# GpSimd's split of a weight unit into high and low parts: the low part written in eight blocks of 128x128 in place of four of 128x256

## The reference, cut to what matters

```python
u = rmsnorm(h, norm_mix[i]);  proj = u @ w_in[i]                  # first block, attention and delta-net inputs
h = h + jnp.concatenate([attn_out, dn_out], axis=-1) @ w_o[i]
gate = jax.nn.sigmoid(rmsnorm(h, norm_ple[i]) @ w_ple_gate[i])
h = h + gate * (p[i] @ w_ple_proj[i])
u = h @ w_in[l];  x = x + jnp.concatenate([y_pool, y_hgrn], axis=-1) @ w_out[l]   # second block
```

## Time and profile before

| | |
|---|---|
| median of 3 runs | 2493.02 us (2489.05 to 2496.16) |
| the profiled execution: its own time | 2492.07 us |
| the span of its trace | 2490.3 us |
| TensorE busy | 2387.1 us (96% of the span) |
| VectorE busy | 1842.2 us (74%) |
| GpSimd busy | 1267.7 us (51%) |
| ScalarE busy | 943.6 us (38%) |
| mean granted TensorE clock | 0.99 of full |

### The profile page before, as it was taken

How to read it: one execution, slowest core, us unless ns; L and a number is a source line. 1 busy time by engine, 2 the same in 40 slices (tenths; PEclk the granted TensorE clock), 3 DMA queues, 4 the chain that set the end, 5 groups by cost and what they waited for, 6 DMA issues and landing times.

```text
span 2490.3 us, 38938 instructions
## 1 busy us (share of the span) xinstructions
PE 2387.1 (96%) x15284; PEld 1893.9 (76%) x15284; DVE 1842.2 (74%) x2356; ACT 943.6 (38%) x1488; POOL 1267.7 (51%) x1143
## 2 busy tenths in 40 slices
PE   8888999999999999999999999999999999999997
PEld 6766777777778877878777778787777877778885
DVE  3676565647877898888946777778487777888887
ACT  3154223315333344344424344444153333444433
POOL 4622333545555545544467656556655555455442
PEclk9998999999999999999999999999999999999998
DMA  4200101210444474434122111111314444744432
GB/s 156 77 18 18 36 22 33 85 52 32 142 142 163 156 255 169 169 111 143 52 68 85 54 35 35 35 44 49 107 40 148 161 149 147 239 163 152 136 126 95
DMA packets 109709, 254.99 MB, mean 102 GB/s; under 512 B 9312, under 2 KB 9568, under 8 KB 107360
## 3 DMA queue, kind: packets, MB, share of 16 engines
q1 hardware_dynamic: 104112, 233.82, 27.7%
q10 hardware_dynamic: 5424, 18.75, 2.2%
HBM read 182.28 MB, written 67.63 MB: 100 GB/s over the span
## 4 chain that ended last, share of the span: by engine, by line
PE 32%; DVE 12%; issue 3%; ACT 1%; POOL 1%; DMA 1%; SPq 0%; DVEq 0%; ACTq 0%; POOLq 0%
PE pairs L687 22%; PE mid L687 10%; DVE work L1757 2%; DVE tmp L1757 2%; DVE res L1757 2%; DVE work_r L1757 2%; DMA w_raw<-w_up 1%; DVE w_raw L1757 1%; DVE tmp L2176 1%; DVE work L2143 1%; POOL w_hi L650 0%; DVE x_lo L1761 0%; POOL w_lo L654 0%; DVE res L2632 0%; DVE x_lo_raw L1757 0%
## 5 line engine op out<-in xcount | busy, mean ns | idle before, releaser
L687 PE MATMUL pairs<-x_hi,w_hi 128*128 128x512 f32 x1592 | 544.5, 406 | 31.8 <-DVE x_lo L1761 14.0
L687 PE MATMUL pairs<-x_lo,w_hi 128*128 128x512 f32 x1592 | 528.6, 396 | 0.5 <-issue 0.5
L687 PE MATMUL pairs<-x_hi,w_lo 128*128 128x512 f32 x1592 | 525.4, 394 | 1.1 <-issue 1.1
L687 PEld LDWEIGHTS pairs<-x_hi,w_hi 128*128 128x128 f32 x1592 | 285.4, 190 | 117.0 <-issue 37.7
L670 POOL TENSOR_TENSOR w_lo<-w_raw,w_hi 128x512 fp32r<-128x512 f32 x150 | 237.9, 1595 | 221.2 <-ACT w_hi L1284 221.1
L687 PEld LDWEIGHTS pairs<-x_hi,w_lo 128*128 128x128 f32 x1592 | 297.9, 189 | 64.5 <-issue 1.2
L687 PEld LDWEIGHTS pairs<-x_lo,w_hi 128*128 128x128 f32 x1592 | 297.0, 189 | 62.5 <-issue 1.3
L687 PE MATMUL pairs<-work_r,w_hi 128*128 128x512 f32 x1072 | 330.1, 392 | 5.1 <-DVE work_r L1757 2.1
L687 PE MATMUL mid<-work_r,w_hi 128*128 128x512 f32 x992 | 311.2, 395 | 17.0 <-DVE work_r L1757 12.1
L654 POOL TENSOR_TENSOR w_lo<-w_raw,w_hi 128x256 fp32r<-128x256 f32 x312 | 314.6, 1039 | 6.5
L647 POOL TENSOR_TENSOR idle<-idle 128x1 f32<-128x1 f32 x78 | 20.1, 258 | 563.6 <-PE pairs L687 554.7
(11 more groups left out here) (217 smaller groups left out, 3876.0 us busy)
## 6 DMA issues: line engine op xcount, KB each, us to landing
h_ops<-work SPq DMA_DIRECT2D x224, 256.0 KB, 4.4
w_raw<-w_stream SPq DMA_DIRECT2D x81, 512.0 KB, 3.5
w_raw<-w_up SPq DMA_DIRECT2D x120, 256.0 KB, 3.9
out_sq<-h_ops SPq DMA_DIRECT2D x28, 1024.0 KB, 5.1
x_lo_raw<-h_ops SPq DMA_DIRECT2D x28, 1024.0 KB, 5.1
work<-w_down SPq DMA_DIRECT2D x16, 1024.0 KB, 6.7
out_sq<-w_down SPq DMA_DIRECT2D x8, 1024.0 KB, 7.3
x_lo_raw<-w_down SPq DMA_DIRECT2D x8, 1024.0 KB, 5.4
```

What stands on the lines that cost most here:

```text
L687: return nc.tensor.matmul(out, w, x, start=start, stop=stop)
```

## The change

The four instructions that write `w_lo` in `split` become eight, of 128 columns each. The last one raises `w_split` as before. The four that write `w_hi` stay as they are, as does every wait.

```diff
             PIECES = [slice(n * QUARTER, (n + 1) * QUARTER) for n in range(4)]
+            TILES = [slice(n * P, (n + 1) * P) for n in range(KT)]
...
-                for part in PIECES:
+                for part in TILES:
                     ins = nc.gpsimd.tensor_tensor(w_lo[:, slot, part], w_raw[:, slot, part], w_hi[:, slot, part], ALU.subtract)
                 ins.then_inc(w_split, 1)
```

## The result

The changed kernel takes **2500.05 us** (median of 19 runs, 2495.25 to 2511.14). The kernel before, in the same comparison, takes 2492.52 us (19 runs, 2484.60 to 2502.28). The ratio is **1.003 [1.002, 1.004]**, so the change costs 7.5 us, with an interval of 5 to 10. The forecast was +1.2 us, with 2488 to 2502 as its range. The time lies inside the range, at its upper end, but the sum was far too small, and "no change that can be measured" did not come true: 19 runs of each tell the two kernels apart. What holds the time is the width of the range. The profiled execution took 2505.18 us, a slow one of the 19. A second profiled execution of the same kernel took 2498.52 us.

The account below looks back on a forecast made before the run. TensorE's matmuls, with some 100 us of holes, were taken to bound the kernel. The terms 1.5 + 1.1 - 1.0 - 0.4 gave +1.2 us, on the median 2493.02 + 1.2 = 2494.2 us, range 2488 to 2502.

Parts of the forecast that it names:

- The price of an instruction and the quiet split: On GpSimd, 460 ns for a 128-column piece; an undisturbed split grows by 0.57 us, nearly all of it hidden.
- The gate unit: Last four units of the gate product: split grows by 0.57 us, 0.3 us of slack stays, so 0.
- The heads of the earlier trace: Five splits in the heads: 0.57 + 1.2 = 1.8 us later against 1.94 us of slack, so 0, barely.
- The pooling split: Split with 0.24 us of slack, ending at 1399.86: grows by 0.57 + 1.0, TensorE opens the unit about 1.3 us late.
- The first split: Already waited for by TensorE: 0.57 us more, plus 1.0 for meeting the `x_lo` operation, +1.5 us (bounds 0.57 and 2.6).
- 2 x 0.57: Two waited-for splits of the last output product, with no further turns against VectorE: +1.1 us (bounds 1.1 and 3.1).
- This wait takes it up: TensorE's 3.0 us wait for VectorE's `small`, at 1432 us, absorbs the 1.3 us of lateness from near 1400: 0.
- SyncE's reload: Reload of the slot starts later by the split's growth, lands in 3.5 us, is needed over 9 us later: nothing.
- VectorE's gain of 1.4 us: Shorter pieces give VectorE 0.25 us back per old meeting: -1.0 us in the wait for `small`, -0.4 us elsewhere.
- the faster rival: Shorter pieces give VectorE 21 us back, nearly half of it on the path: 2485.6 us, chance 0.08.
- The slower one: Slack of heads and gate used up, pooling lateness not absorbed, VectorE gains nothing: +9.8, 2502.8 us, chance 0.13.
- The third rival: Pieces of 128 overlap wholly, without the fixed cost; quiet splits stay at 2.8 us: 2492.5 us, sharing the forecast's 0.79.

Follow-up runs that it names:

- experiment 2: Kernel before with `w_lo` in eight pieces in all splits but the first, which keeps four: 2497.59 us, ratio 1.0026.
- 11: Kernel before with `w_lo` in eight pieces in the last output product's splits alone, four elsewhere: 2494.90 us, ratio 1.0018.
- experiment 1: Kernel before with `w_lo` in eight pieces in the first split alone, four elsewhere: 2490.87 us against 2490.64, ratio 1.0005.
- 3: Kernel before, `w_lo` still in four pieces, with four one-column additions of two SBUF inputs among them in each split: 2496.45 us, ratio 1.0028.
- 7: Kernel before with `w_lo` in two pieces of 512 columns in all splits: 2494.93 us, ratio 1.0019.
- 8: Kernel before with `w_lo` in one instruction of 1024 columns in all splits: 2499.99 us, ratio 1.0042.
- 4: Kernel before, `w_lo` still in four pieces, with four memsets of 96 columns among them in each split: 2495.38 us, ratio 1.0019.

## Why the prediction was right or wrong

**Right, to 0.1 us.** The price of an instruction and the quiet split: 462 ns and 3.38 us, for 460 and 3.38. The gate unit: slack 0.33 us (0.3 predicted), `tmp` pair 2.88 (2.95), so that a meeting gave VectorE 0.28 us back, not 0.25. The heads of the earlier trace rows: low part from 4.28 to 6.01 us, +1.73 for 1.8, slack 0.2 and no wait. The pooling split: +1.52 for 1.57. The seventh unit of the last output product: the gap between matmuls grew from 0.07 us to 0.63, +0.56 for 0.57. `w_lo` at 395.0 us lies inside the 360 to 400 foretold.

**Wrong, term by term.** The mechanism named there (fixed cost of an instruction, turns with VectorE, TensorE waiting where there is no slack) is what the traces show. The sum failed in the terms below. TensorE's waits on the split were foretold at 4 to 5 us and are 6.6 and 7.5, and the matmul foretold at 21.7 us came at 22.30.

- *The first split*, predicted +1.5: TensorE's wait grew by 1.77 us, within the bound of 2.6. Of the split's growth of 2.12 us, 1.55 are meetings where I counted 1.0.
- *"2 x 0.57" for the last output product.* The second unit's term was mis-sized. I wrote that VectorE goes on with operations that take no turns. That holds for what is in line at the old end, but late pieces meet the `work` operations behind it. The wait grew by 1.43 us in the first profile, by 2.4 in the second (3.58 us) and by 2.1 in experiments 2 and 11.
- *"This wait takes it up"* for the 1.3 us of the pooling split. TensorE waited 0.96 us there and the wait for `small` gave back only 0.3. VectorE did run ahead by 3.3 us in the stretch up to 1410 us, compared with how late TensorE was (7.4 us behind the trace of before), but then stood waiting for ScalarE's `state` and had lost its lead at 1422 us: the row

```profile
1422.40 0.69 DVE L1758 TENSOR_TENSOR state<-state,work 128x512 f32<-128x512 f32 x1 [2.51 <-ACT state L1285]
```

- *SyncE's reload, "nothing".* The prediction looked at when TensorE needs the next unit in the slot. Behind the last split the slot takes `w_up`, which VectorE needs at once. That split grew by 2.35 us (6.18 to 8.53), VectorE waits 1.15 us for the load, and TensorE 1.0 us more for VectorE. The start of the first MLP adds 0.3 and 0.2 us of TensorE's wait for `work` in the two profiles; why is not shown.
- *VectorE's gain of 1.4 us.* VectorE got 16 us of busy time back (21 us were worked out in the faster rival), but TensorE's waits behind it shrank by no more than the 0.3 us of `small`. In the first block's heads it went the other way: three waits for `state`, 1.0 us, where a small VectorE operation in the chain of the recurrence is late.
- *The clock* had no term at all. A longer pause of TensorE can have a stretch at 1.2 GHz behind it, as at 23 and 1747 us. At the first place the clock fell in the three traces with a wait of 2.37 to 2.73 us (the change twice, experiment 1) and stayed up in the eleven with 1.60 us or less. At the second it fell behind waits of 2.62, 3.29 and 3.19 us (the first profile, 2, 3) and stayed up behind 3.58 and 3.31. Over the 19 runs the mean granted clock was 0.9881. Over 93 runs of the kernel before, in the comparisons of the experiments, it was between 0.9895 and 0.9901, and their times rise by about 1700 us per unit of clock lost (correlation -0.68). The cleanest pair is experiment 2 and its own before, 0.9887 and 0.9895. The change's 0.9881 lies 0.0014 to 0.0020 lower. A loss of 0.0008 to 0.0020 is 1.4 to 3.4 us, an estimate from this correlation, not a thing that an experiment separated.

The sum by measured terms, first and second profile of the change: waits on the split +4.8 and +5.7 us, `state` +1.0 and +1.0, `work` at the start of the two MLPs +1.3 and +1.2, `small` -0.3 and -0.4, in all **+6.8 and +7.5 us, beside 7.5 in the runs** (5 to 10). The clock's 1.4 to 3.4 us would come on top, 8.2 to 10.9, and the longer waits for "issue" in the first block with it. The pairs of traces differ by 13.1 and 13.4 us, more than the runs do. So the waits alone are enough, and how much of the clock and of "issue" belongs to the change stays open.

**The rivals.** The slower one gave 2502.8 us, near the 2500.05 measured, but for a reason that didn't happen: no gate unit and no head of the earlier trace rows waits for its split. It shares two of its parts with what happened: the pooling split isn't taken up, and VectorE's gain isn't won. The faster rival fell: waits on VectorE did not shrink. Half of its rule is real all the same, as experiments 7 and 8 show in reverse: longer pieces do cost VectorE time, and TensorE with it. From four pieces to eight VectorE still gains, but TensorE's new waits are more. The third rival fell with the 462 ns.

The exclusive lock of the Trainium skill (SBUF - State Buffer, the section on SBUF's layout and its two sides) agrees with experiments 3 and 4: a one-column addition with two SBUF inputs waits for a whole turn of VectorE, and a memset doesn't.

## What to carry to other kernels

When an operation of GpSimd with two SBUF inputs runs beside a busy VectorE, count turns before elements. Each instruction more costs GpSimd up to one whole VectorE instruction (1.0 us here), each longer one costs VectorE, and the best size lies between (four pieces here, with 0.42%, 0.19% and 0.30% lost at one, two and eight). A split that is late meets what comes next on VectorE, so look past the old end when you size it. Ask of every split what its slot is loaded with next and who waits for that load; the last one before a new stage is easily missed. Allow for a fall of the clock behind a longer pause of TensorE, and don't read a stretch at half clock as the edit's before a kernel unchanged there has been seen without it.

## What was not expected of the hardware

- A one-column addition on GpSimd of 194 ns took 437 ns on average among the pieces (x312), while a memset of 96 columns took 177 ns on average at the same places, also beside VectorE.
- The same instructions, behind the same pause of TensorE (2.25 to 2.27 us, near 475 us of the span), ran at the full clock in five traces and fell to half in nine. Behind a pause of 3.58 us near 1744 us the clock stayed up, and behind one of 2.62 us at the same place it fell. The time at half clock was 44.9 and 52.9 us in two traces of the very same kernel.
- TensorE stood for "issue" inside its stretches of small matmuls for 6.0 to 11.2 us in all, with the longest single one between 1.7 and 2.4 us, differing from execution to execution of the same kernel. They tend to be longer where the splits of the first block's loop have eight instructions (7.7 to 11.2 us, beside 6.0 to 8.0). What the engine waits for there no view shows, and it stays open.
